# Mixture-of-experts encoder: result rows scattered to their tokens, plain loads in the combine, and another order for the first loads

## The chip, the cores and the metric

The kernel runs on one core of a Trainium2 chip. Such a core has a matrix engine (TensorE, PE in the rows), a vector engine (VectorE, DVE), a scalar engine (ScalarE, ACT), GpSimd (POOL) and a sync engine (SyncE, SP) that here only issues transfers. The engines run their own instruction lists and wait for each other through semaphores. Transfers between DRAM and the on-chip memory run on 16 DMA engines, which all queues share. In the rows, queue q1 holds what SyncE issues, q10 what ScalarE issues, and q0 what GpSimd issues.

The metric is the device time of the whole program in microseconds (us). Lower is better.

## The reference

The input is one sequence of 512 tokens with 1024 float32 values each. Two layers follow one another, and each is a mixer and a mixture of experts, with an RMS norm ahead of either:

```
for layer in range(2):
    h = rms_norm(x, norm_mix_g[layer])
    mix = hybrid_retention_s5(h, ...) if layer % 2 == 0 else windowed_gqa(h, ...)
    x = x + mix
    h = rms_norm(x, norm_ffn_g[layer])
    x = x + hier_moe(h, ...)
return rms_norm(x, norm_final_g)
```

`hier_moe` picks one of 4 groups for each token and in it the best 2 of 8 experts. An expert is `(silu(xb @ w_gate[e]) * (xb @ w_up[e])) @ w_down[e]`, with matrices of 1024x512, 1024x512 and 512x1024. The two results of a token are weighted by their gates and added to x. With 32 experts and 1024 assignments of a token to an expert, an expert has 32 tokens on average.

## The kernel before

The x matrix stays on the chip as 4 tiles of 128 tokens (`xv`). A norm (`act_norm_tile`, `dve_norm_tile`) goes tile by tile: ScalarE squares and sums, VectorE scales, ScalarE takes the root, VectorE multiplies, TensorE transposes into `hT`, and ScalarE and VectorE evacuate.

The program starts with the norm of layer 0's mixer. SyncE's list begins with one load of all of x, the constant table `c_tab`, six loads of small parameters and then the first two weight slots (`sp_mixer0`). GpSimd loads the norm's gain. After the norm TensorE makes the u projection (L1507, weights in slot 0) and z blocks (L1527), while VectorE computes the tables of the S5 part from `c_tab` and the small parameters. GpSimd starts its own part when those tables are ready. Ahead of it, GpSimd fills the rows of `y_dram` that belong to overflow blocks with ones (L2067).

In the mixture of experts (`*_moe`) each expert is one block of up to 64 tokens. 15 more overflow blocks exist for experts with more than 64 tokens, in a loop that runs no time with these inputs. All tokens' normed rows are in `h_dram`. The router (`dve_router`, `pe_router`) makes for each block the list of its tokens (`SLL`), padded with an index that is out of bounds. It does that as a product of one-hot matrices on TensorE (L397). For each block e:

- GpSimd copies the block's column of the list (L883) and issues a gather of its rows from `h_dram` (L890). Rows out of bounds are skipped.
- TensorE transposes them (L580), multiplies by gate and up (L588, L589), transposes the product (L594) and multiplies by down (L601). ScalarE and VectorE evacuate; the last evacuation (L742) makes `YE`, in which partitions 0 to 63 hold the first half of a result row and partitions 64 to 127 the second.
- ScalarE stores all 64 rows of `YE` in two transfers of 64x512 to the block's own place in `y_dram` (L871), used or not.
- SyncE loads the weights of block e+2 into the ring slots that block e has left (L795): gate and up once `e_gu` says that their matmuls are done, down once `e_dn` does. Blocks 0, 1 and 2 are loaded ahead, block 2 into places of its own. So blocks 3 and 4 are the first whose loads wait for matmuls of block 0 and 1.

When all stores have landed, GpSimd issues 8 gathers from `y_dram` (L920), one for each tile and each of the two choices, with indices that VectorE computed at the router's end (`ROWI`, L547 to L564). VectorE adds them to x (`dve_combine`, L933) and starts the next norm. SyncE has by then issued the next layer's first two weight slots (L2005).

Of the kernel before, what the change touches and what calls it, by code (L numbers as in the profile page):

```python
# [31 lines left out]
RH = 4  # L32
# [30 lines left out]
for _name, _w in [("ident", P), ("cos", NT * 64), ("sin", NT * 64), ("relp", P), ("relm", P), ("pos", 4),  # L63
                  ("before", P), ("eye16", GC), ("gtie", NGRP), ("etie", EPG), ("eid", BLK), ("bidx", MAXOV + 1),
                  ("tok", NT), ("place", BLK)]:
# [14 lines left out]
def shape_constants():  # L80
# [25 lines left out]
    put("place", (i // 4 + 16 * ((i % 4 - i // 16) % 4))[None, :])  # L106
    b = np.zeros((32, 2 * S), np.float32)
# [6 lines left out]
def encoder(nc, A, out):  # L114
    ctx = ExitStack()
    with ctx:
# [49 lines left out]
        y_dram = dram("y_dram", [NBLK * BLK, D])  # L166
# [19 lines left out]
        def spm(i):  # L186
# [4 lines left out]
        c_in, x_in, gn_in, s5_in, cc_in, b_in, moe_in = (sem(n) for n in (  # L191
            "consts_loaded", "x_loaded", "gain_loaded", "s5_rows_loaded", "s5_c_loaded", "s5_b_loaded", "router_loaded"))
        fill_st = sem("y_rows_filled")

        pe_passed, pool_passed, sp_passed = (sem(n) for n in ("pe_wait_passed", "pool_wait_passed", "sp_wait_passed"))
# [56 lines left out]
        def act_norm_tile(act, A_, n, t, ready):  # L252

            ss = small_norm(n)
            ready(act, t)
# [6 lines left out]
        NS_T = sb("norm_small", 16)  # L262
# [4 lines left out]
        def dve_norm_tile(dve, V, n, t):  # L267
# [7 lines left out]
            if t == 0:  # L275
                dve.wait_ge(gn_in, 16 * (n + 1))
# [71 lines left out]
        ROWI = INTS[:, 0:8]  # L348
# [4 lines left out]
        STG = [INTS[0:BLK, 64 + NBLK + b:65 + NBLK + b] for b in range(2)]  # L353
        assert 20 + MAXOV + 2 <= 64
# [7 lines left out]
        g_L, g_Lm, g_sl = Count("router_places"), Count("router_lists_mm"), Count("router_lists")  # L362
        xg_ld = [sem(f"x_block{b}") for b in range(2)]
# [5 lines left out]
        yk_ld = [sem(f"y_rows{i}") for i in range(8)]  # L369
# [16 lines left out]
        def pe_router(pe, l):  # L386
# [11 lines left out]
            i.then_inc(g_Lm.s, 1)  # L398

# [31 lines left out]
        def dve_router(dve, l, V):  # L431
# [98 lines left out]
            bl = shp(BL1, 8, NBLK)  # L530
            V(tv.tensor_tensor(shp(PL1, 8, BLK), ins_dim(rt("pos"), 2, BLK), ins_dim(cst("place"), 1, 8), ALU.is_equal))
            V(tv.tensor_tensor(bl, ins_dim(rt("ob"), 2, NBLK), ins_dim(cst("eid")[:, 0:NBLK], 1, 8), ALU.is_equal))
            V.sync()
            for k in range(2):
                V(tv.tensor_tensor(bl[:, NT * k:NT * (k + 1)], bl[:, NT * k:NT * (k + 1)], ins_dim(cst("tok"), 2, NBLK),
                                   ALU.mult), g_L if k else None)
            V(tv.tensor_tensor(rt("cle").rearrange("p (b e) -> p b e", e=NE), ins_dim(rt("inc"), 1, MAXOV + 1),
# [7 lines left out]

# [23 lines left out]
        def overflow_blocks(eng, l, body):  # L569

# [1590 lines left out]
```

## Time and profile before

| | us |
|---|---|
| median of 3 runs | 1761.19 |
| lowest, highest | 1756.18, 1762.73 |
| the profiled execution's own time | 1760.08 |
| its span in the profile | 1758.0 |

| engine | busy us | share of the span |
|---|---|---|
| TensorE | 1412.1 | 80% |
| VectorE | 543.7 | 31% |
| ScalarE | 247.2 | 14% |
| GpSimd | 172.9 | 10% |

The profile is of one execution. Its span is cut into stages by what runs: layer 0's mixer to about 390 us, its router to 421, its experts to 920, the combine and layer 1's mixer to 1196, the router to 1226, the experts to 1726, and the combine with the final norm to the end. A share of busy time is an average over all of them. The queues moved 486.05 MB in all, 440.26 MB of them on q1. In a timeline row the first number is the start, the second the time from the start of the first to the end of the last of the instructions merged into it, and the bracket tells how long the engine was idle before and what ended that. In a row of a DMA queue, the last number is the time that its packets took, as a share of 16 engines over the stretch that was asked for.

### The profile page before, as it was taken

To read this page: it belongs to the slowest core of one execution; us is meant where nothing else is said; L and a number is where in the kernel's file an instruction comes from. 1 tells how busy PE (TensorE), PEld (TensorE's weight loads), DVE (VectorE), ACT (ScalarE), POOL (GpSimd) and SP (SyncE) were. 2 spreads that over 40 slices of the span, in tenths; PEclk is the share of its full clock that TensorE was granted. 3 is DMA by queue.
4 is the path that set the end of the run, shared out by engine and by line. 5 is a ranking of instruction groups with operands and counts; after the bars stand their busy time and mean duration, and the time that the engine had idled before them with its cause. 6 is when DMAs were issued, how large, how long until landed. Compare 5 with 4: busy or idle time off the path is not lost. (4 is left out here: it accounts for less than half of the span.)

```text
span 1758.0 us, 18695 instructions
## 1 busy us (share of the span) xinstructions
PE 1412.1 (80%) x7013; PEld 686.5 (39%) x7013; DVE 543.7 (31%) x1125; ACT 247.2 (14%) x501; POOL 172.9 (10%) x215
## 2 busy tenths in 40 slices
PE   6999756995988878878875989894997878878872
PEld 3444745552333333323322457653333323323330
DVE  6998589124111111101114038424111101101104
ACT  2201222110100000000002027411100000000001
POOL 0007070001100000000002000001100000000002
PEclk9999877996999999989997989996999989989996
DMA  7510502426999999999996200406899999999994
GB/s 236 150 66 15 49 13 97 203 101 264 392 403 413 404 410 413 410 404 410 407 395 231 80 17 1 192 36 255 348 392 411 409 407 410 408 403 412 405 418 168
DMA packets 75027, 486.05 MB, mean 276 GB/s; under 512 B 16752, under 2 KB 23536, under 8 KB 50016
## 3 DMA queue, kind: packets, MB, share of 16 engines
q1 hardware_dynamic: 53984, 440.26, 63.5%
q0 software_dynamic: 9472, 23.94, 4.3%
q10 hardware_dynamic: 11520, 21.15, 3.2%
q8 instruction: 34, 0.56, 0.1%
q14 instruction: 17, 0.14, 0.0%
HBM read 465.91 MB, written 27.79 MB: 281 GB/s over the span
## 5 line engine op out<-in xcount | busy, mean ns | idle before, releaser
L588 PE MATMUL psum<-ring,work 128*64 128x512 f32 x992 | 494.9, 657 | 128.4 <-DMA ring<-in_moe_w_up 125.7
L589 PE MATMUL psum<-ring,work 128*64 128x512 f32 x992 | 495.9, 658 | 0.0
L588 PEld LDWEIGHTS psum<-ring,work 128*64 128x64 f32 x992 | 145.1, 151 | 449.8 <-issue 446.2
L601 PE MATMUL psum<-ring,work 128*64 128x512 f32 x992 | 226.5, 598 | 31.1 <-DVE work L739 31.1
L736 DVE TENSOR_TENSOR work<-work,psum 64x512 f32<-64x512 f32 x64 | 44.2, 690 | 639.4 <-ACT work L693 566.4
L693 ACT ACTIVATE work<-psum 64x512 f32<-64x512 f32 x64 | 37.8, 590 | 839.9 <-PE psum L589 839.9
L589 PEld LDWEIGHTS psum<-ring,work 128*64 128x64 f32 x992 | 145.0, 151 | 0.0
L601 PEld LDWEIGHTS psum<-ring,work 128*64 128x64 f32 x992 | 66.6, 136 | 145.0 <-issue 125.1
L742 DVE COPY work<-psum 128x512 f32<-128x512 f32 x64 | 44.2, 691 | 247.7 <-PE psum L601 247.7
L1527 PE MATMUL psum<-ring,hT 128*128 128x512 f32 x256 | 112.1, 600 | 2.1 <-ACT work L1646 2.1
L883 POOL COPY ints<-ints 64x1 uint32 (+1 forms) x64 | 11.4, 178 | 816.6 <-PE psum L580 772.8
L1527 PEld LDWEIGHTS psum<-ring,hT 128*128 128x128 f32 x256 | 49.0, 192 | 63.8 <-issue 63.8
L580 PE MATMUL psum<-consts,work 64*128 64x64 f32 x512 | 67.2, 272 | 7.0 <-DMA work<-h_dram,ints 7.0
L890 POOL DMA_INDIRECT work<-h_dram,ints x64 | 61.4, 959 | 54.6 <-POOL ints L883 54.6
L580 PEld LDWEIGHTS psum<-consts,work 64*128 64x128 f32 x512 | 62.7, 204 | 10.5 <-DMA work<-h_dram,ints 8.9
L308 PE MATMUL psum<-consts,work 128*128 128x128 f32 x128 | 23.7, 347 | 43.6 <-DVE work L277 43.6
L1889 PE MATMUL psum<-ring,hT 128*128 128x512 f32 x128 | 56.2, 594 | 0.5 <-issue 0.5
L1810 PE MATMUL psum<-hT,ring 128*64 128x512 f32 x256 | 55.2, 592 | 0.9 <-ACT hT L294 0.9
L594 PEld LDWEIGHTS psum<-consts,work 64*128 64x128 f32 x256 | 35.4, 210 | 51.9 <-issue 51.9
L690 ACT COPY work<-psum 128x512 f32<-128x512 f32 x64 | 37.5, 585 | 96.4 <-PE psum L580 96.4
L1853 PE MATMUL psum<-work 128*128 128x128 f32 x320 | 41.7, 288 | 5.4 <-DVE work L1987 5.4
L594 PE MATMUL psum<-consts,work 64*128 64x64 f32 x256 | 44.2, 293 | 0.0
(350 smaller groups left out, 1422.2 us busy)
## 6 DMA issues: line engine op xcount, KB each, us to landing
ring<-in_moe_w_gate SPq DMA_DIRECT2D x62, 2048.0 KB
ring<-in_moe_w_up SPq DMA_DIRECT2D x62, 2048.0 KB, 23.1
ring<-in_moe_w_down SPq DMA_DIRECT2D x62, 2048.0 KB, 23.6
y_dram<-work ACTq DMA_DIRECT2D x128, 128.0 KB
ring<-in_hyb_w_in SPq DMA_DIRECT2D x5, 2048.0 KB, 9.8
ring<-in_swa_w_qkv SPq DMA_DIRECT2D x3, 2048.0 KB, 14.3
y_dram<-ones POOLq DMA_DIRECT2D x1, 4096.0 KB, 19.9
ring<-in_hyb_w_out SPq DMA_DIRECT2D x2, 2048.0 KB, 7.7
```

The source lines that it names most:

```text
L580: i = nc.tensor.transpose(bank[b][:, c * BLK:(c + 1) * BLK], XG[b][:, c::KC], ident[0:BLK, 0:BLK])
L588: nc.tensor.matmul(bank[2 + b][0:BLK, :], XT[b][:, c, :], g[:, c, :], start=c == 0, stop=c == KC - 1)
L589: i = nc.tensor.matmul(bank[2 + b][BLK:P, :], XT[b][:, c, :], u[:, c, :], start=c == 0, stop=c == KC - 1)
L594: i = nc.tensor.transpose(bank[4 + b][:, c * BLK:(c + 1) * BLK], HD[b][:, c::HC], ident[0:BLK, 0:BLK])
L601: i = nc.tensor.matmul(bank[6 + b][BLK * hf:BLK * (hf + 1), :], HTE[b][:, c, :], d[:, c, hf * HALF:(hf + 1) * HALF], start=c == 0, stop=c ...
L736: nc.vector.tensor_tensor(HD[b], AA[b], bank[2 + b][BLK:P, :], ALU.mult).then_inc(done, 1)
L742: nc.vector.tensor_copy(YE[b], bank[6 + b][:, :]).then_inc(done, 1)
L890: pool.indirect_dma_start(XG[b], None, h_dram, bass.IndirectOffsetOnAxis(STG[b], 0), bounds_check=S - 1, oob_is_err=False).then_inc(done, 16)
L1527: x = nc.tensor.matmul(bank[i % 4], hT[:, c, t * P:(t + 1) * P], w[:, c, :], start=c == 0, stop=c == KC - 1)
L1810: x = nc.tensor.matmul(bank[i][64 * hf:64 * hf + 64, :], w[:, c, 64 * (2 * k + hf):64 * (2 * k + hf) + 64], hT[:, c, :], start=c == 0, sto ...
L1853: x = nc.tensor.matmul(bank[4 + kb][:, k * P:(k + 1) * P], SBF[it % 4][:, BAND * k + kb * P:BAND * k + (kb + 1) * P], DG[it % 2][:, k * P: ...
L1889: x = nc.tensor.matmul(b, hT[:, c, t * P:(t + 1) * P], wo[n][:, c, :], start=c == 0, stop=c == KC - 1)
```

## The change

The results of an expert no longer go to the block's own rows. `y_dram` now has a place for each token, choice and half row: 2048 rows of 512 values. The router makes a second list, `SCL`, of 128 rows for each block (partition and half row), by 16 more matmuls on TensorE whose one-hot side carries twice the token's row (`srow`). GpSimd copies the block's column and issues an indirect store, a scatter, of `YE`. Rows out of bounds are skipped. The fill with ones and the computation of `ROWI` on VectorE go. In the combine SyncE issues 8 plain loads of 128x1024.

At the start, x comes in four loads with the identity behind the first; the first norm's gain comes from ScalarE's queue; the rest of the constant table and four small parameters come from GpSimd's; two small parameters stand behind the weights. In every norm a square root of one value stands ahead of the wait for the first tile.

```
+            if t == 0:
+                A_(nc.scalar.activation(WARM, ONES[:, 0:1], ACT.Sqrt))
             ready(act, t)
...
+            bs = shp(BL2, 8, NBLK)
+            pe.wait_ge(g_S.s, l + 1)
+            for hf in range(2):
+                for a in range(8):
+                    i = nc.tensor.matmul(bank[5][BLK * hf:BLK * (hf + 1), 0:NBLK], pl[:, a, :], bs[:, a, :], start=a == 0,
+                                         stop=a == 7)
+            i.then_inc(g_Sm.s, 1)
...
+            V.sync()
+            V(tv.tensor_tensor(bs, bs, ins_dim(cst("srow"), 2, NBLK), ALU.mult), g_S)
...
-            pi, a, b = rt("q").bitcast(I32), rt("qp").bitcast(I32), rt("ei").bitcast(I32)
...
-            V(tv.tensor_copy(ROWI, rt("row")))
...
+            dve.wait_ge(g_Sm.s, l + 1)
+            V(tv.tensor_scalar(SCL, bank[5][:, 0:NBLK], cst("half"), 2.0 * NOROW, ALU.add, ALU.add), g_sc)
...
-            def store(e, par):
-                act.wait_ge(e_y, b0 + e + 1)
-                store_y1(act, par, e, y_st[par])
...
+            def scatter_y(b, done):
+
+                pool.indirect_dma_start(y_dram, bass.IndirectOffsetOnAxis(SSTG[b], 0), YE[b], None, bounds_check=4 * S - 1,
+                                        oob_is_err=False).then_inc(done, 16)
+
+            def store(e, par):
+                pool.wait_ge(e_y, b0 + e + 1)
+                col = SCL[:, e:e + 1] if isinstance(e, int) else SCL[:, bass.ds(e, 1)]
+                pool.tensor_copy(SSTG[par], col).then_inc(e_sst, 1)
+                pool.wait_ge(e_sst, b0 + e + 1)
+                pool.sem_inc(passed, 1)
+                scatter_y(par, y_st[par])
...
+            for t in range(NT):
+                for k in range(2):
+                    r0 = 2 * (S * k + P * t)
+                    sp.dma_start(YK[NT * k + t], y_dram[r0:r0 + 2 * P, :].rearrange("(p h) d -> p (h d)", h=2)).then_inc(
+                        yk_ld[t] if t + k else yk0_ld, 16)
...
-            for i in (k * NT + t for t in range(NT) for k in range(2)):
-                pool.indirect_dma_start(YK[i], None, y_dram, bass.IndirectOffsetOnAxis(ROWI[:, i:i + 1], 0)).then_inc(yk_ld[i], 16)
...
-            sp.dma_start(xv, A["x"][0].rearrange("(t p) d -> p t d", p=P)).then_inc(x_in, 16)
+            for t in range(NT):
+                sp.dma_start(xv[:, t, :], A["x"][0, t * P:(t + 1) * P, :]).then_inc(x_in[t], 16)
+                if t == 0:
+                    sp.dma_start(ident, A["c_tab"][:, 0:P]).then_inc(id_in, 16)
...
+            pool.dma_start(CT[:, P:], A["c_tab"][:, P:]).then_inc(c_in, 16)
...
-            pool.dma_start(y_dram[NE * BLK:].rearrange("(p r) (c d) -> p (r c) d", p=P, d=P), ins_dim(ONES[:, :], 1, n)).then_inc(
-                fill_st, 16)
-            pool.wait_ge(fill_st, 16)
...
+            act.dma_start(GN[:, :], bass.AP(A["norm_mix_g"].tensor, 0, [[0, P], [1, D]])).then_inc(id_in, 16)
```

SyncE's list at the start of the program, before:

```order
2 L1729 DMA x_sb<-in_x 128x4x1024
3 L1734 DMA consts<-in_c_tab 128x1204
4 L1735 DMA work<-in_s_a_re 32x128
5 L1736 DMA work<-in_s_a_im 32x128
6 L1737 DMA s_small<-in_s_log_step 32x2
7 L1738 DMA s_small<-in_ret_decay_logit 128x8
8 L1739 DMA s_small<-in_s_d 128x4x1
9 L1740 DMA s_small<-in_s_b_glu 128x4
10 L1732 DMA ring<-in_hyb_w_in 128x8x512 x2
11 L1750 DMA work<-in_s_c_re 128x1x64 x8
```

And of the changed kernel:

```order
2 L1739 DMA x_sb<-in_x 128x1024
3 L1741 DMA consts<-in_c_tab 128x128
4 L1739 DMA x_sb<-in_x 128x1024 x3
5 L1744 DMA ring<-in_hyb_w_in 128x8x512 x2
6 L1748 DMA s_small<-in_s_d 128x4x1
7 L1749 DMA s_small<-in_s_b_glu 128x4
8 L1757 DMA work<-in_s_c_re 128x1x64 x8
```

Nothing but x and the identity stands ahead of the first weights now, and x is four semaphores instead of one.

TensorE's list from the router's product to the first expert's matmuls (layer 0), before. The 64x48 matmuls make the lists, the 16x512 one belongs to layer 1's attention bias, the 128x64 ones transpose block 0's rows:

```order
141 L390 MATMUL psum<-work,ones 128x160
142 L391 MATMUL psum<-work,consts 128x128
143 L397 MATMUL psum<-work 64x48 x8
144 L2117 MATMUL psum<-work 16x512
145 L580 MATMUL psum<-consts,work 128x64 x8
```

And of the changed kernel:

```order
141 L399 MATMUL psum<-work,ones 128x160
142 L400 MATMUL psum<-work,consts 128x128
143 L406 MATMUL psum<-work 64x48 x8
144 L413 MATMUL psum<-work 64x48 x16
145 L2125 MATMUL psum<-work 16x512
146 L585 MATMUL psum<-consts,work 128x64 x8
```

The 16 matmuls of the second list stand between the first list and block 0's transposes.

GpSimd's list in the loop over the blocks (layer 0), before; one of the two halves of the loop's body:

```order
72 L883 COPY ints<-ints 64x1
73 L884 REGISTER_ALU
74 L890 DMA work<-h_dram,ints 64x1024
```

And of the changed kernel:

```order
79 L878 COPY ints<-ints 64x1
80 L879 REGISTER_ALU
81 L885 DMA work<-h_dram,ints 64x1024
82 L900 REGISTER_ALU
83 L902 ISA
84 L902 COPY ints<-work 128x1
85 L896 DMA y_dram<-work,ints 2048x512
```

The gather of block e+4 is followed by the scatter of block e, which waits for `YE` of that block.

## Rows read from the trace of the kernel before

**Rows 1.** Waits from 500 to 850 us: who waited, us in total, times, longest.

```profile
PE psum L588 <- DMA ring<-in_moe_w_up: 52.0, 19, 5.3
```

**Rows 2.** Same stretch: length, PE, PEld, DVE, ACT, POOL, PEclk, DMA share, GB/s.

```profile
500.00:850.00 350.00, 286.18 (x1298) 115.40 (x1294) 39.71 (x66) 25.87 (x44) 24.96 (x44) 0.92 1.01 409
```

**Rows 3.** DMA packets and queues from 433 to 901 us.

```profile
DMA packets 19264, 190.72 MB, mean 408 GB/s; under 512 B 3676, under 2 KB 3676, under 8 KB 8320
...
q10 hardware_dynamic: 4640, 7.61, 4.3%
...
q0 software_dynamic: 2320, 3.82, 2.5%
```

**Rows 4.** DMA queue 0 from 55 to 85 us, the fill of y_dram.

```profile
q0 software_dynamic: 1040, 4.19, 50.3%
```

**Rows 5.** GpSimd's timeline between two blocks.

```profile
504.64 0.96 POOL L890 DMA_INDIRECT work<-h_dram,ints  x1 [0.85 <-POOL ints L883]
```

**Rows 6.** Timeline of the start, to the first projection.

```profile
10.29 1.06 ACT L258 ACTIVATE work<-x_sb 128x1024 f32<-128x1024 f32 x1 [8.27 <-DMA x_sb<-in_x]
...
11.45 1.28 ACT L260 ACT_TABLE_LOAD   x1
...
13.25 1.28 DVE L277 SCALAR_TENSOR_TENSOR work<-x_sb,norm_small,norm_gain 128x1024 f32<-128x1024 f32 x1
...
18.99 1.29 DVE L277 SCALAR_TENSOR_TENSOR work<-x_sb,norm_small,norm_gain 128x1024 f32<-128x1024 f32 x1
...
23.46 29.45 PE L1507 MATMUL psum<-ring,hT 128*64 128x512 f32 x128 [0.35 <-DVE ring L1677]
```

**Rows 7.** Transfers by line, whole run: count, KB each, us from issue to landing.

```profile
h_dram<-work ACTq DMA_DIRECT2D x8, 512.0 KB, 2.6
...
norm_gain<-in_norm_mix_g POOLq DMA_DIRECT2D x2, 512.0 KB, 10.2
```

**Rows 8.** Busy time and transfers of the first 18 us.

```profile
0.00:18.00 18.00, 3.32 (x15) 3.07 (x16) 4.27 (x9) 7.44 (x13) 1.14 (x6) 1.00 0.85 311
```

**Rows 9.** VectorE's waits from 20 to 400 us, one of them.

```profile
DVE work L1196 <- PE psum L1553: 5.4, 1, 5.4
```

**Rows 10.** Timeline of layer 1's combine.

```profile
1725.20 0.69 DVE L742 COPY work<-psum 128x512 f32<-128x512 f32 x1 [3.76 <-PE psum L601]
...
1730.39 0.97 POOL L920 DMA_INDIRECT work<-y_dram,ints  x1 [60.48 <-issue]
...
1734.80 1.28 DVE L933 SCALAR_TENSOR_TENSOR x_sb<-work,x_sb 128x1024 f32<-128x1024 f32 x1 [8.91 <-DMA work<-y_dram,ints]
...
1741.93 0.15 DVE L271 TENSOR_SCALAR norm_small<-norm_small 128x1 f32<-128x1 f32 x1
```

**Rows 11.** TensorE from the router's lists to block 0, layers 0 and 1.

```profile
412.45 1.94 PE L397 MATMUL psum<-work 128*64 128x48 f32 x16 [7.75 <-DVE work L535]
...
414.32 1.89 PE L2117 MATMUL psum<-work 32*16 32x512 f32 x2
...
418.95 1.14 PE L580 MATMUL psum<-consts,work 64*128 64x64 f32 x8 [2.75 <-DMA work<-h_dram,ints]
...
1218.46 1.94 PE L397 MATMUL psum<-work 128*64 128x48 f32 x16 [7.75 <-DVE work L535]
...
1224.62 1.14 PE L580 MATMUL psum<-consts,work 64*128 64x64 f32 x8 [4.21 <-DMA work<-h_dram,ints]
```

**Rows 12.** Busy time by stretch: block 0's gate and up, slow and fast.

```profile
420.00:426.00 6.00, 5.33 (x15) 1.53 (x16) 0.00 (x0) 1.87 (x2) 1.13 (x2) 0.50 0.98 371
...
427.00:431.00 4.00, 4.00 (x20) 1.23 (x17) 0.00 (x0) 0.13 (x1) 0.00 (x0) 1.00 0.00 0
```

**Rows 13.** SyncE's first load that waits for block 0.

```profile
430.86 0.33 SPq L795 DMA_DIRECT2D ring<-in_moe_w_gate  x1
```

**Rows 14.** TensorE after an idle time in layer 0's mixer.

```profile
247.11 0.70 PE L1458 MATMUL psum<-ring,work 128*64 128x128 f32 x4 [8.36 <-DVE hT L1437]
...
252.78 1.09 PE L1464 MATMUL psum<-ring,hT 64*64 64x128 f32 x16
```

More of the change, by code:

```diff
@@ L190, in encoder @@
         w_in = [sem(f"w_loaded{i}") for i in range(6)]
[L191 to L195, printed above, removed]
+        c_in, id_in, gn_in, s5_in, cc_in, b_in, moe_in = (sem(n) for n in (
+            "consts_loaded", "ident_and_first_gain_loaded", "gain_loaded", "s5_rows_loaded", "s5_c_loaded", "s5_b_loaded", "router_loaded"))
+        passed = sem("wait_passed")
+        x_in = [sem(f"x_tile{t}_loaded") for t in range(NT)]
         class Count:
@@ L353, in encoder @@
         STG = [INTS[0:BLK, 64 + NBLK + b:65 + NBLK + b] for b in range(2)]
+        BL2 = cut(WK, 12288 + 8 * NBLK, 8 * NBLK)
+        SCL = rt("big")[:, 0:NBLK].bitcast(U32)
+        SSTG = [INTS[:, b:b + 1] for b in range(2)]
         assert 20 + MAXOV + 2 <= 64
@@ L368, in encoder @@
         y_st = [sem(f"y_stored{b}") for b in range(2)]
-        yk_ld = [sem(f"y_rows{i}") for i in range(8)]
+        yk_ld = [sem(f"y_rows{t}") for t in range(NT)]
+        yk0_ld = sem("y_rows_first")
         ov = [{k: sem(f"ov{l}_{k}") for k in ("w", "i", "xg", "xt", "xe", "gu", "a", "h", "ht", "he", "dn", "y", "st")}
@@ L720, in act_moe @@
                     xe(i * 2 + 2 + k, k)
-                    store(i * 2 + k, k)
                     silu(i * 2 + 2 + k, k)
-            for b in range(2):
-                store(NE - 2 + b, b)
             def body(j):
@@ L898, in pool_moe @@
             pool.wait_ge(h_st, 16 * NT * (l + 1))
+            def scatter_y(b, done):
[6 more added lines that the diff above has]
+                pool.wait_ge(e_sst, b0 + e + 1)
+                pool.sem_inc(passed, 1)
+                scatter_y(par, y_st[par])
             fetch(0, 0)
             fetch(1, 1)
-            with pool.Fori(0, (NE - 2) // 2) as i:
+            fetch(2, 0)
+            fetch(3, 1)
+            pool.wait_ge(g_sc.s, l + 1)
+            with pool.Fori(0, (NE - 4) // 2) as i:
                 for k in range(2):
-                    fetch(i * 2 + 2 + k, k)
+                    fetch(i * 2 + 4 + k, k)
+                    store(i * 2 + k, k)
+            for e in range(NE - 4, NE):
+                store(e, e % 2)
             def body(j):
@@ L908, in body @@
                 pool.tensor_copy(STG[1], SLL[:, bass.ds(j + NE, 1)]).then_inc(o["i"], 1)
[L909 to L910 removed]
+                pool.wait_ge(o["i"], j * 2 + 1)
+                pool.sem_inc(passed, 1)
                 gather_x(1, o["xg"])
[L912 to L926 removed]
+                pool.wait_ge(o["y"], j + 1)
+                pool.tensor_copy(SSTG[1], SCL[:, bass.ds(j + NE, 1)]).then_inc(o["i"], 1)
+                pool.wait_ge(o["i"], j * 2 + 2)
+                pool.sem_inc(passed, 1)
+                scatter_y(1, o["st"])
+                pool.wait_ge(o["st"], j * 16 + 16)
+                pool.sem_inc(passed, 1)
+            overflow_blocks(pool, l, body)
         def dve_combine(dve, l, V):
@@ L1490, in pe_mixer0 @@
         def pe_mixer0(pe):
-            pe.wait_ge(c_in, 16)
+            pe.wait_ge(id_in, 32)
             pe_norm(pe, 0)
```

115 lines of the change are left out of this document (42 added, 73 removed).

## Prediction

> **What bounds the kernel now.** I read the waits, then busy time by stretch, the DMA queues and the timelines of the seams. In the expert stages the transfers bind: from 500 to 850 us TensorE waits 19 times for an up matrix, 52.0 us in all [rows 1], the DMA share is 1.01 at 409 GB/s, and VectorE, ScalarE and GpSimd are busy for 7 to 11% [rows 2]. There a byte or packet less is time gained. Outside them, the program is a chain of engine work, in which a shift of the beginning moves everything behind it.
>
> **Scatter instead of stores.** From 433 to 901 us (468 us) 29 blocks pass: queue 10 has 58 stores, each of 64 packets of 2 KB and 16 that signal, 58 x 80 = 4640; queue 0 has 29 gathers of 64 + 16 packets, 2320 [rows 3]. 3.82 MB are 32 rows of 4 KB per gather, so a skipped row is a small packet and not nothing. The stores hold 4.3% x 468 / 29 = 0.694 us of the 16 engines per block, the gathers 2.5% x 468 / 29 = 0.403. With a for a 2 KB packet and s for a small one (a 4 KB row counted as 2a), 128a + 32s = 11.10 and 64a + 48s = 6.45 engine-us, so s = 0.028 and a = 0.080. A scatter has 64 of the one and 64 + 16 of the other: 7.36 engine-us, 0.46 us. The ends: by bytes alone 131 KB at 409 GB/s, 0.32 us; by the gather's mean packet, 0.403 x 144 / 80 = 0.725 us. The nearest row for writing to y_dram through queue 0 is the fill: 4.19 MB in 50.3% of 30 us, 236 ns per packet of 4 KB and engine [rows 4], by which a scatter would be (64 x 118 + 80 x 28) / 16 = 612 ns. I take 0.50, nearer to the packets that were measured beside the weights. 0.194 us saved x 58 blocks of both layers = **-11.3 us**; ends -21.7 and +1.8.
> The page "DMA: Bandwidth & Descriptors" of the Trainium skill, section "Bandwidth", speaks against the change: it puts a floor of some 10.5 ns on each packet of a transfer, by which a scatter's 144 packets would be 1.5 us. The trace does not bear that out: a gather's 80 packets would by it be 0.84 us and hold 0.403. By the page's figure the sum would be 58 x 0.8 = 47 us on the slow side.
> What the scatter costs GpSimd is hidden: a copy of some 0.2, a gap of 0.85 and an issue of 0.96 us [rows 5], twice per block of 16.4 us. Queued behind its wait for `YE` is the gather of block e+5, which can start only a block later in any case. The buffer of `YE` is wanted again two blocks on. ScalarE loses its issues, and it waits anyway. The fill that goes lay beside TensorE's 82 us of z projections: nothing.
>
> **The start.** Today x lands at 10.29; squaring and a table load of 1.28 put the first product at 13.25, the fourth ends at 20.28 (1.91 apart), and the projection starts 3.2 later, at 23.46 [rows 6]. Afterwards tile 0 is alone at the front: a transfer of its size takes 2.6 us [rows 7]; beside the gain's I put it at 5.0. The table load is before the wait, so the product comes 1.7 later, at 6.7, if the gain is there (10.2 us on GpSimd's queue [rows 7]; I take that it lands by 6.7 as the second of two transfers at the front). The fourth product ends at 6.7 + 1.28 + 5.73 = 13.7, and the chain allows 16.9. But slot 0's weights come behind x, the identity, the gain and the table: 5.33 MB. The first 18 us moved 311 GB/s, 5.6 MB [rows 8], at some 390 at the end, so they land at 17.3. The projection starts there: **-6.2 us**; ends -8.5 (no gap in the stream) and -3.
> It shifts what follows only if VectorE's tables come with it. They end 5.4 us before the wait on L1553 is over [rows 9]; by the same timeline TensorE gets to that product 1.6 us after they end. They need the table from GpSimd's queue, issued at about 4; by 10.2 [rows 7] it lands at 14.5, in time for 17.3. The later small parameters are not read before 70 us.
> The root ahead of the wait in the other four norms is worth nothing: their table load lies beside VectorE's two sums of the second tile, and the next root comes after these.
>
> **The combines.** Today the last `YE` is ready at 1725.89, the first gather is issued at 1730.39 and the first sum starts at 1734.80, 4.4 after the issue; the norm's step follows at 1741.93 [rows 10]. Afterwards: copy and gap make it 1727.0, the scatter lands 4.4 later at 1731.4, a plain load 2.6 later at 1734.1. The second tile waits for four loads, three more at 1.3 us (0.52 MB at 409 GB/s): 1738.0, and two sums end at 1740.6. So -1.3 for each layer, **-2.7**; ends -5 (SyncE wakes as fast as an engine) and +2 (a scatter into DRAM signals 2 us later than a gather).
>
> **The router.** On VectorE the added product of 128x384 lies in the time in which it waits for TensorE's list, and about 2 us of index arithmetic go from a place where no one waits. On TensorE 16 more matmuls, 32 instructions at 1.94 / 16 = 0.12 us: 3.9 us. In layer 0 they and L2117 (1.89) stand before block 0's transposes, which now come 2.74 after L2117's end [rows 11]: **+1.2**. In layer 1 there are 4.21 us of idle time [rows 11]: nothing.
> But TensorE's clock is 0.50 (1.2 GHz) in block 0's gate and up, 420 to 426, and 1.00 from 427 on [rows 12], after a router in which it mostly idled. The transfers stand still meanwhile (0 GB/s), since the first load that waits for block 0 is issued at 430.86 [rows 13]. So a faster block 0 starts the stream of weights earlier. At 1.00 a pair of matmuls takes about 0.43 us (some 20 matmuls in 4.00 us [rows 12]), at 0.50 twice that; the 6.3 us up to the rise hold some seven slow pairs, so 3.0 us are at stake. After the change TensorE works from 412.45 [rows 11] without a pause of over 1 us. After an idle 8.36 us the slow form lasted 5.7 us of work on narrow matmuls [rows 14], and the new work is 8 us in layer 0 and 6 in layer 1 before gate and up. So I take the fast form: **-6.0** for two layers; ends 0 and -6.5.
> The page "TensorE: Matmul & The Clock Gate", section "Part 1: The HAM clock gate", of the Trainium skill has it that recent activity, and not a count of instructions, raises the clock. Rows 14 agree; whether matmuls as small as the list's raise it, no row shows.
>
> **Sum.** -11.3 - 6.2 - 2.7 + 1.2 - 6.0 = -25.0 against the profiled execution's 1760.1 (span 1758.0 and 2.1 around it): 1735.1. It lies 1.1 under the median, so 1736 for the median.
>
> **The rivals.**
> A, the clock does not rise for the narrow matmuls, 22%: the 6.0 go, 1742. For it: the list's matmuls are small. Against: rows 14.
> B, scatters hold the engines as long as the stores did, or the rows are moved whether skipped or not (128 x 80 + 16 x 28 ns over 16 are 0.67 us), 14%: 11.3 become 0 to -1.8 the other way, about 1748. The fill's slow packets speak for it, the gathers' small ones against it.
> C, the parameters on GpSimd's queue come so late that VectorE's tables hold TensorE at 140 us, 8%: the -6.2 go, 1742. The 10.2 us of a gain on that queue speak for it.
> D, slower, 5%: the descriptors of queue 0 are dear for the engines. If a gather's 32 rows carried all of its 0.403 us, one would be 202 ns, and with 128 such a scatter 1.61 us; that is +0.92 x 58 = 53 less the other terms' 13.7, so 1800. It decides from 0.694 + 13.7 / 58 = 0.93 us per scatter on. Against it is that 48 of a gather's 80 packets move nothing and yet the whole fits in 0.403. The Trainium skill's floor per packet, named above, would land in the same place.
> The forecast itself has 48%, its own range 1729 to 1745. 3% are left for what I don't see.
>
> **Range and chances.** What a measurement here can tell from no change is 0.5%, 8.8 us. A and B together give 1754. The range 1724 to 1754 leaves out D and the outer ends. Faster by over 0.5% (under 1752.4) hold the forecast, A, C and most of B, less what is unseen: 0.83. Within 0.5%: the rest of B and combinations of A to C, 0.10. Slower: D and an unseen wait, 0.07.
>
> **What would show it.** Right: a spacing of gate loads about 0.2 us shorter (468 us for 29 blocks become about 462), queue 0 at 5.6% and queue 10 empty in that stretch, the first projection at 17.3, the step of the last combine 15 us after the last `YE`, and a clock of 1.00 in block 0's gate and up. Wrong: queue 0 above 7%, waits of TensorE for VectorE at 140 us, GpSimd's gathers later than TensorE wants them, or a combine that waits longer for SyncE's loads than for the gathers now.

## The result, and the profile after

| | before | after |
|---|---|---|
| median, us | 1761.19 | 1744.96 |
| lowest, highest of five | 1756.18, 1762.73 | 1739.70, 1748.02 |
| span of the profiled execution | 1758.0 | 1741.8 |

The ratio of the times is 0.9913, with a 95% interval from 0.9886 to 0.9940: 16.2 us faster, where 25 were forecast. The two profiled spans differ by 16.2 us too, so the two traces can be laid side by side. I cut both at the same events and took the differences:

| stretch | before | after | difference |
|---|---|---|---|
| start to the u projection | 23.46 | 19.91 | -3.55 |
| u projection to layer 0's lists | 388.99 | 388.89 | -0.10 |
| lists to block 0's gate and up | 8.32 | 8.62 | +0.30 |
| block 0's gate and up, to the first dependent load | 10.09 | 8.73 | -1.36 |
| that load to the end of the last `YE` | 487.87 | 481.95 | -5.92 |
| last `YE` to layer 1's first projection | 31.71 | 30.47 | -1.24 |
| that projection to layer 1's lists | 268.02 | 270.59 | +2.57 |
| lists to block 0's gate and up | 7.97 | 8.09 | +0.12 |
| block 0's gate and up | 10.04 | 9.87 | -0.17 |
| first dependent load to the last `YE` | 489.42 | 484.11 | -5.31 |
| last `YE` to the end | 32.11 | 30.57 | -1.54 |
| sum | 1758.00 | 1741.80 | -16.20 |

The gain sits where the scatter replaced the stores (-11.2), at the start (-3.6) and in the combines (-2.8). Block 0's two stretches, which the clock was to shorten, brought 1.5 of the 6 forecast, and a stretch that the change does not touch lost 2.6. This is one pair of profiles. Over the nine profiles of kernels with the changed TensorE list (this one and eight of the runs below), block 0's gate and up take 9.0 us on average in layer 0 (8.7 to 10.0) and 9.8 in layer 1 (8.8 to 10.1), so the 1.5 stands within some tenths; of the kernel before there is one profile.

The expert stages are bound as before, by the transfers. This is the wait of TensorE for an up matrix from 500 to 850 us:

```profile
PE psum L593 <- DMA ring<-in_moe_w_up: 52.0, 19, 4.7
```

And this the busy time by engine of that stretch (columns as in [rows 2]):

```profile
500.00:850.00 350.00, 287.57 (x1298) 115.23 (x1296) 38.63 (x64) 24.73 (x42) 51.53 (x87) 0.92 1.01 408
```

The wait is the same 52.0 us as in [rows 1], the DMA share is 1.01 again, and GpSimd is now busy for 15% instead of 7, which no other engine's wait in that stretch is put down to. What has changed is what fills the engines. These are the queues from 433 to 901 us, as in [rows 3]:

```profile
DMA packets 17858, 189.66 MB, mean 405 GB/s; under 512 B 3713, under 2 KB 3713, under 8 KB 6849
...
q1 hardware_dynamic: 13149, 181.86, 95.7%
q0 software_dynamic: 4705, 7.74, 4.8%
```

Queue 10 is empty, queue 0 has doubled its bytes, and both together fell from 6.8% to 4.8%. In the same 468 us the weights' queue moved 181.86 MB instead of 179.23.

The start, with the rows that answer to [rows 6]: the squares of the four tiles on ScalarE, the fourth product on VectorE, and the projection.

```profile
6.04 1.06 ACT L261 ACTIVATE work<-x_sb 128x1024 f32<-128x1024 f32 x1 [3.37 <-DMA x_sb<-in_x]
...
9.45 1.06 ACT L261 ACTIVATE work<-x_sb 128x1024 f32<-128x1024 f32 x1 [1.83 <-DMA x_sb<-in_x]
...
11.22 1.06 ACT L261 ACTIVATE work<-x_sb 128x1024 f32<-128x1024 f32 x1 [0.20 <-DMA x_sb<-in_x]
...
13.52 1.06 ACT L261 ACTIVATE work<-x_sb 128x1024 f32<-128x1024 f32 x1 [0.58 <-DMA x_sb<-in_x]
...
15.42 1.28 DVE L281 SCALAR_TENSOR_TENSOR work<-x_sb,norm_small,norm_gain 128x1024 f32<-128x1024 f32 x1
...
19.91 27.75 PE L1518 MATMUL psum<-ring,hT 128*64 128x512 f32 x128 [0.35 <-DVE ring L1688]
```

Each square names x as what it waited for. The tiles land 1.8 to 3.4 us apart, so the fourth product ends at 16.70, and the projection follows 3.2 us later as before. It does not wait for its weights. The first product came at 7.91, 1.2 us after the forecast's 6.7, and the fourth starts 7.5 us behind it, not 5.7.

Layer 1's combine, against [rows 10]: the last `YE`, its scatter, the loads, the first sums and the norm's step.

```profile
1710.54 0.69 DVE L740 COPY work<-psum 128x512 f32<-128x512 f32 x1 [3.76 <-PE psum L606]
...
1712.34 0.99 POOL L896 DMA_INDIRECT y_dram<-work,ints  x1 [0.86 <-POOL ints L902]
...
1715.05 4.58 SPq L865 DMA_DIRECT2D work<-y_dram  x8
...
1718.67 2.63 DVE L944 SCALAR_TENSOR_TENSOR x_sb<-work,x_sb 128x1024 f32<-128x1024 f32 x2 [7.44 <-DMA work<-y_dram]
...
1725.73 0.15 DVE L275 TENSOR_SCALAR norm_small<-norm_small 128x1 f32<-128x1 f32 x1
```

From the end of `YE` to the norm's step it is 14.5 us instead of 16.04.

The clock, in the busy times by stretch (columns as in [rows 2]): block 0's gate and up in layer 0, slow and then fast, the same in layer 1, and the first matmuls of layer 1's first projection.

```profile
417.40:420.40 3.00, 2.98 (x8) 1.01 (x10) 0.00 (x0) 1.27 (x1) 0.97 (x1) 0.50 0.90 368
421.00:425.00 4.00, 4.00 (x20) 1.26 (x18) 0.00 (x0) 0.00 (x0) 0.00 (x0) 1.00 0.34 137
1217.20:1222.20 5.00, 4.95 (x12) 1.48 (x14) 0.00 (x0) 1.28 (x1) 0.96 (x1) 0.50 0.94 384
1223.00:1227.00 4.00, 4.00 (x20) 1.12 (x16) 0.00 (x0) 0.00 (x0) 0.00 (x0) 1.00 0.02 6
938.60:942.60 4.00, 4.00 (x10) 1.34 (x12) 0.00 (x0) 0.00 (x0) 0.40 (x1) 0.50 0.84 315
```

The column of 0.50 and 1.00 is the granted clock (1.2 and 2.4 GHz). Layer 0's block 0 has 3.3 slow us instead of 6.0 [rows 12], layer 1's 5.5 instead of 5.9. The last row is new. Before the change the same matmuls ran in the fast form:

```profile
950.40:954.40 4.00, 3.96 (x20) 1.68 (x22) 0.00 (x0) 0.00 (x0) 0.78 (x2) 1.00 0.88 328
```

These are 20 matmuls in 4 us where now there are 10, though the same transposes stand ahead of them in both programs. From 938.57 to 942.9 that is 2.2 of the 2.6 us lost in that stretch. Whether it happens is not set by the program. Of the nine profiles with the changed TensorE list, five have the projection's first 3.2 to 4.4 us at 1.2 GHz and take 269.5 to 270.6 us to layer 1's lists; four have none and take 268.1 to 268.6. The kernel before took 268.0, without slow matmuls there.

### The profile page after: what moved, and what is told of

It is laid out like the page before. It is cut to its first block and busy times, and to the rows that moved or that the text cites. A ratio compares the mean times of both kernels' runs of the same rounds, so it can differ in the third digit from the quotient of the medians.

```text
span 1741.8 us, 18784 instructions
## 1 busy us (share of the span) xinstructions
PE 1416.1 (81%) x7077; PEld 689.7 (40%) x7077; DVE 542.4 (31%) x1109; ACT 247.4 (14%) x505; POOL 230.6 (13%) x330
## 5 line engine op out<-in xcount | busy, mean ns | idle before, releaser
L896 POOL DMA_INDIRECT y_dram<-work,ints x64 | 65.5, 1023 | 56.6 <-POOL ints L902 55.5
L585 PE MATMUL psum<-consts,work 64*128 64x64 f32 x512 | 67.3, 273 | 1.3 <-DMA work<-h_dram,ints 1.3
```

Source lines behind the costliest of these rows:

```text
L585: i = nc.tensor.transpose(bank[b][:, c * BLK:(c + 1) * BLK], XG[b][:, c::KC], ident[0:BLK, 0:BLK])
L896: pool.indirect_dma_start(y_dram, bass.IndirectOffsetOnAxis(SSTG[b], 0), YE[b], None, bounds_check=4 * S - 1, oob_is_err=False).then_inc(d ...
```

## The experiments

All but after_again are edits of the changed kernel. Each was timed beside the kernel before, and its ratio to that is given. "Stretch" is the time from block 0's first dependent load to the end of the last `YE`.

### ScalarE's stores again (stores_back)

```
+            def store(e, par):
+                act.wait_ge(e_y, b0 + e + 1)
+                store_y1(act, par, e, y_st[par])
...
-                    store(i * 2 + k, k)
```

> The changed kernel with ScalarE's two plain stores per block in place of the scatter, into the block's own rows; the combine's plain loads stay, so the sums take wrong rows. Theory 1 (what a block's result costs the DMA engines sets the expert stages): the two stretches from block 0's first dependent load to the last YE are 5.9 and 5.3 us longer than in the changed kernel (482 and 484 us become 488 and 489), the time is some 11 us above it, about 1756, less 1 to 2 since the last stores signal earlier than a scatter. Rival (the stages gained by something else, such as the work taken from ScalarE or the earlier start of the stream): the stretches stay at 482 and 484 and the time within 3 us of 1745.

Measured: 1757.14 us, ratio 0.9973 (0.9963 to 0.9982), and stretches of 489.66 and 489.93 us. Taking the scatter out costs 12 to 13 us against the changed kernel's two medians (1744.96, 1743.73), and the two stretches of the profiles are 13.5 longer. Theory 1 holds against the start, which stayed as changed. It does not settle ScalarE's list, since the stores are on ScalarE again here. The run with no row skipped, below, does: its ScalarE list is the light one, and its layer 0 stretch is 489.1 us, within 0.6 of the 489.66 with stores. So it is the skipped rows that made the expert stages faster.

### What a scatter's rows cost (rows_skipped, all_rows)

```
-                pool.indirect_dma_start(y_dram, ..., YE[b], None, bounds_check=4 * S - 1,
+                pool.indirect_dma_start(y_dram, ..., YE[b], None, bounds_check=0,
```

> The changed kernel in which every scatter skips all rows but at most one (its bound is 0), with y_dram filled with ones ahead under the z projections; the sums take these ones. Theory 1 (what the rows of a scatter move is what it costs, at about 0.28 us of the 16 engines per block): the expert stretches shrink by up to 0.28 x 25 = 7 us each, to 475 and 477, time 1731 to 1737. Rival A (a skipped row costs as much as a row): no change, 482 and 484, 1745. Rival B (the stretch no longer hangs on the transfers alone): less than 3 us per layer, 1739 to 1745.

```
-            V(tv.tensor_scalar(SCL, bank[5][:, 0:NBLK], cst("half"), 2.0 * NOROW, ALU.add, ALU.add), g_sc)
+            V(tv.tensor_scalar(SCL[:, 0:NE], cst("alt"), cst("half"), 0.0, ALU.add, ALU.add), g_sc)
```

> The changed kernel whose scatters skip nothing: block e writes all 128 partitions to rows 128 (e mod 16) and on; y_dram is filled with ones ahead, and the combine's sums are of no use, so only layer 0's expert stretch is read. Theory 1 (the queue's packets carry two rows each, 64 and 16 signals per scatter; rows that move cost about 0.28 us per 64 of 2 KB, of which 0.6 come back as time): the scatter's packets carry 262 KB, and the stretch from the first dependent load to the last YE is 487 to 489 us instead of 482, as far above as it was below (477.5) with all rows skipped. Rival A (packets count, not what they carry): 482. Rival B (by bytes at 409 GB/s in full, 0.32 us for each of 28 blocks): 491.

Layer 0's stretch is 477.53 us with all rows skipped (first load 427.90, last `YE` 905.43) and 489.12 with none skipped. Between them lie 481.95 in the changed kernel and 481.8 to 483.0, mean 482.4, over the six profiles of kernels with this scatter and no edit of TensorE's list. The whole time of rows_skipped, 2001 us, says nothing on the scatter: with other sums layer 1's router chose other experts, and its overflow blocks ran (gate loads 40 us apart at the end, which no other kernel has). all_rows took 1756.6 us, ratio 0.9970 (0.9957 to 0.9982).

Each of the two runs has one profile, and the six range over 1.2 us.

The queues from 440 to 880 us (packets, MB, share of 16 engines); of the changed kernel:

```profile
DMA packets 16260, 178.22 MB, mean 405 GB/s; under 512 B 3538, under 2 KB 3538, under 8 KB 5840
...
q0 software_dynamic: 4542, 7.51, 4.9%
```

with all rows skipped:

```profile
DMA packets 16428, 176.48 MB, mean 401 GB/s; under 512 B 4976, under 2 KB 4976, under 8 KB 5885
...
q0 software_dynamic: 4560, 3.74, 3.0%
```

and with none skipped:

```profile
DMA packets 16021, 179.18 MB, mean 407 GB/s; under 512 B 3060, under 2 KB 3060, under 8 KB 5760
...
q0 software_dynamic: 4480, 11.07, 6.8%
```

The packets are the same number, some 28.4 times 160: 80 for the gather, and 80 for the scatter of 128 rows, not 144. The bytes run from nothing over 131 to 262 KB per scatter, so a packet carries up to two rows, and one whose rows are both skipped is small. The sizes in the trace's packet records show it directly. In the changed kernel a scatter has some 16 data packets of 4096 bytes, 33 of 2052 and 16 of 8, and with all rows skipped all but one of the data packets have 8 bytes. In the records of this stretch a packet of 4 or 8 bytes takes 9 to 10 ns, a stored row of 2048 bytes 84 ns before the change, and a gathered row of 4096 bytes 188 ns. With the gathers' 2.6% taken off (queue 0 of the kernel before in this stretch), a scatter holds the 16 engines for 3.0 - 2.6 = 0.4% of 440 us / 28.5 = 0.06 us with no rows, 2.3% / 28.4 = 0.36 with half of them, and 4.2% / 28 = 0.66 with all. The time follows by less. The 31 scatters of a stretch are 9.3 us of engine time from none to half and 9.3 from half to all; the stretch grew by 4.9 and 6.7. Theory 1 holds in both runs, and Rival A fails in both; in all_rows the measured 489.1 lies between it and Rival B.

Where the rest of the freed time goes, the gate loads show in part. The first five gaps between them are the same before and after, 71.3 us in all: the fifth load after the first comes at

```profile
502.12 0.33 SPq L795 DMA_DIRECT2D ring<-in_moe_w_gate  x1
```

before (430.86 + 71.3), and after the change (426.15 + 71.3) at

```profile
497.40 0.33 SPq L793 DMA_DIRECT2D ring<-in_moe_w_gate  x1
```

In layer 0 these five gaps are 71.3 to 71.4 us in all 14 profiles, whatever a scatter moves. So 15% of a stretch does not hang on it. The 23 gaps behind them sum to 364.2 us with all rows skipped, to 367.9 to 369.3 in the six profiles (mean 368.5) and to 376.0 with none skipped. That is 4.4 and 7.5 us for 23 x 0.30 = 6.9 us of engine time each: 0.6 and 1.1 of it, 0.86 together. In the middle of the stretch, then, most of the freed time is gained, and part of the shortfall lies in the blocks at its front.

### The start (front_old, front_old2, table_after_x)

```
+            sp.dma_start(xv, A["x"][0].rearrange("(t p) d -> p t d", p=P)).then_inc(x_in[0], 16)
+            sp.dma_start(CT[:, :], A["c_tab"]).then_inc(c_in, 16)
...
+            gain(0)
```

> The changed kernel with the first loads as they were before (x in one load, the whole table and the small parameters on SyncE's queue, the gain on GpSimd's); scatter, combine and router as changed. Theory 1 (a shift of the start is carried through to the end): the u projection starts near 23.5 us instead of 19.9, the router's lists near 412.4 instead of 408.8, and the time is 3.6 us above the changed kernel, about 1748.6, ratio to before 0.993. Rival (the earlier start is eaten later): the time is that of the changed kernel, 1745, ratio 0.991.

> Again the changed kernel with the first loads of before, now on the same chip as the changed kernel. By the profiles seen so far its u projection starts 1.7 to 2.5 us later. Theory 1 (that shift reaches the end): 2 to 3 us above the changed kernel of this call. Rival (it does not reach the end): within 1 us of it.

```
+            pool.wait_ge(x_in[NT - 1], 16)
             pool.dma_start(CT[:, P:], A["c_tab"][:, P:]).then_inc(c_in, 16)
```

> The changed kernel with one wait more: GpSimd issues the rest of the constant table only when the fourth tile of x has landed. Theory 1 (x lands late because the table and the gain share the engines with it): the last square starts at 12 instead of 13.5 us, the u projection at 18.5 instead of 19.9, time 1.4 us below the changed kernel, about 1743.6. Rival A (the tiles' own packets set their landing): 19.9 and 1745 as before. Rival B (the table now comes too late for VectorE's own tables): VectorE waits for it, TensorE waits for VectorE near 140 us, and the time is above 1745.

With the old loads the projection starts at 22.38 in both profiles, not at 23.46, since the root ahead of the wait is still there: 1.1 us of the gain at the start are its. With the new loads it starts at 19.9 to 20.7 in eight profiles, so the new order of the loads brings 1.7 to 2.5. The end does not show them clearly. front_old took 1744.58 (ratio 0.9898, 0.9883 to 0.9913), front_old2 1745.60 (0.9897, 0.9881 to 0.9912) beside the changed kernel's 1743.73 (0.9887, 0.9872 to 0.9903). That is 1.9 us with intervals of 2.7 on either side: it fits the shift and it fits none. This stays open.

table_after_x took 1741.36 (0.9892, 0.9878 to 0.9907). That is 2.4 to 3.6 us under the changed kernel's two medians, but each was timed beside other executions of the kernel before, and by the ratios (0.9913 and 0.9887) it is not clear of them. A gain in time is not shown. Its last square, the later issue of the table, and the projection:

```profile
12.30 1.04 ACT L261 ACTIVATE work<-x_sb 128x1024 f32<-128x1024 f32 x1
...
12.33 0.55 POOL L2074 DMA_DIRECT2D consts<-in_c_tab  x1 [8.74 <-DMA x_sb<-in_x]
...
19.47 5.00 PE L1518 MATMUL psum<-ring,hT 128*64 128x512 f32 x22 [0.35 <-DVE ring L1688]
```

The fourth tile lands 1.2 us sooner once the table is out of its way, as Theory 1 had it: its square starts at 12.2 to 12.3 in all three profiles with this edit and at 13.3 to 13.5 in the eight with the new loads and without it. The projection moves by 0.4 to 1.2 us against the other profiles, and VectorE does not come to wait for the table.

### The combine (combine_gathers)

```
-                    sp.dma_start(YK[NT * k + t], y_dram[r0:r0 + 2 * P, :]...)
+                    pool.indirect_dma_start(YK[NT * k + t], None, y_dram..., bass.IndirectOffsetOnAxis(ROWI[:, ...], 0))
```

> The changed kernel with GpSimd's 8 gathers (of the same rows, by a list) in place of SyncE's 8 plain loads in the combine. Theory 1 (a plain load saves what was seen between the two first profiles): from the last YE to the first sum 10.2 us instead of 7.5 to 8.1, the norm's step 1.5 us later, both layers: 2.5 to 3 us above the changed kernel, 1746 to 1748. Rival (the wait for the last scatter is the longer part, the loads save nothing): 1744.

Measured: 1745.42, ratio 0.9913 (0.9898 to 0.9928). Layer 0's last scatter, the first two gathers and the first sum:

```profile
911.49 0.98 POOL L894 DMA_INDIRECT y_dram<-work,ints  x1 [0.86 <-POOL ints L900]
...
915.04 1.00 POOL L937 DMA_INDIRECT work<-y_dram,ints  x1 [2.57 <-DMA y_dram<-work,ints]
...
916.34 0.97 POOL L937 DMA_INDIRECT work<-y_dram,ints  x1 [0.30 <-issue]
...
918.97 1.28 DVE L949 SCALAR_TENSOR_TENSOR x_sb<-work,x_sb 128x1024 f32<-128x1024 f32 x1 [8.59 <-DMA work<-y_dram,ints]
...
927.74 0.15 DVE L275 TENSOR_SCALAR norm_small<-norm_small 128x1 f32<-128x1 f32 x1
```

From the last `YE` to the norm's step are 17.4 us here and 16.7 in layer 1, against 14.6 and 14.5 with plain loads. The eleven profiles with a scatter and plain loads range from 14.1 to 16.0, mean 14.7. The issues are 1.3 us apart, and each tile needs two. So the plain loads are worth 2.0 to 2.7 us per layer by the mean. With gathers, a scatter ahead of them costs about 1 us against the stores (16.1 before); with plain loads there is no such difference (15.05 and 14.54 in stores_back). By the profile Theory 1 holds. The time does not decide: 1745.42 lies between the two forecasts.

### The clock (after_again, warm_all, warm_fit)

> The changed kernel once more, for what differs between two executions of one kernel. Theory 1 (where TensorE's clock falls and rises is not fixed by the program): the two stretches of the expert stages (block 0's first dependent load to the last YE) are again 482 and 484 us within 1.5, while block 0's gate and up (8.7 and 9.9 us in the first profile) and the stretch from the attention's first projection to layer 1's lists (270.6) come out otherwise by 1 to 3 us. Rival (the clock follows the program): these come out within 0.3 us of the first profile. The time is 1745.

Measured: 1743.73, ratio 0.9887 (0.9872 to 0.9903). The stretches are 482.27 and 483.51 as expected. The other two came out closer than expected. Block 0 took 8.83 and 9.94 us, within 0.1 of the first profile, and the projection to layer 1's lists 269.9 instead of 270.6, which speaks for the rival. But front_old and front_old2, which are one program, differ by 1.4 between the projection and the lists of layer 1 (269.5, 268.1) and by 1.1 in layer 1's block 0 (9.85, 8.77). In front_old the projection's first 3.3 us and 5.5 us of block 0 ran at 1.2 GHz, in front_old2 none and 3.3 (block 0 of layer 1 in both). So part of the clock's steps falls otherwise from one execution to the next, by 1 to 2 us per place. The stretch from the u projection to layer 0's lists varies too (388.9 and 390.8; 390.2 and 388.4), but its time at 1.2 GHz does not go with it (83.7, 83.5, 86.4 and 87.4 us), so that cause is open. The Trainium skill has it so as well ("TensorE: Matmul & The Clock Gate", "Part 1: The HAM clock gate"): the chip's observation runs freely of the kernel's start, and the number of slow matmuls varies with the run. The pair of profiles agrees that it varies; on what it hangs, no run here shows.

```
+        def pe_dummies(n, b):
+            for _ in range(n):
+                nc.tensor.matmul(bank[b][:, :], CT[:, 0:P], CT[:, P:5 * P], start=True, stop=True)
```

> The changed kernel with matmuls on TensorE whose product nobody reads, in places where it waits: 8 and 14 in each router, 30 ahead of layer 1's first norm and 5 after its first two tiles. Theory 1 (TensorE's half clock at the start of block 0 and of the attention's first projection costs end time, since the first dependent weight load waits for block 0): clock 1.00 from the first gate matmul on, block 0's gate and up take 6.9 us instead of 8.7 and 9.9, the attention's first projection gets back 2.3 us, the router's lists 1 to 2 us each; time 6 to 9 us below the changed kernel, 1736 to 1739, ratio 0.986 to 0.988. Rival A (the transfers bind whatever block 0 does): the router parts are given back in the expert stage, only the 2.3 us stay, 1743. Rival B (the clock stays low in spite of them, or they run into the work behind them): 1745 to 1755.

Measured: 1759.27, ratio 0.9990 (0.9981 to 0.9998): Rival B. I had priced an unread matmul at 0.43 us, which is the spacing of a pair of half width; one of full width takes 0.87, and layer 0's lists came at 416.30, 7.5 us late. What the run shows of the clock is worth its time. The list's and the bias' matmuls with the first of the transposes, and then block 0:

```profile
416.30:422.30 6.00, 3.98 (x53) 3.00 (x53) 1.32 (x4) 0.00 (x0) 2.36 (x4) 1.00 0.11 31
423.90:429.40 5.50, 5.49 (x14) 1.71 (x16) 0.00 (x0) 1.25 (x1) 0.96 (x1) 0.50 0.85 352
```

Ahead of 416.30 TensorE had worked without a pause from 391.14. Then came 58 matmuls, nearly all narrow, with a wait of 2.0 us ahead of the last 8, and the clock fell at 422.9, before the first gate matmul at 423.91. In the changed kernel's layer 1 the same narrow work goes on from 1209.16 to 1216.6, with a pause of 1.3 us at 1214.1, and the clock is still 0.50 at 1222.

That is not the rule, though. The nine profiles with the changed TensorE list hold 18 such places, and in 8 of them the clock rose to 2.4 GHz 3.5 to 5.0 us after the first of the list's matmuls and fell again at block 0, from 1.4 us before its first gate matmul to 0.1 behind it. In the other 10 it stayed at 1.2 GHz into block 0. This is after_again in layer 1: the lists, their end with the transposes, and block 0.

```profile
1211.90:1215.40 3.50, 3.50 (x37) 3.50 (x38) 2.20 (x6) 0.00 (x0) 0.33 (x2) 0.50 0.40 169
1215.60:1218.80 3.20, 1.28 (x17) 1.15 (x16) 0.27 (x1) 0.00 (x0) 1.82 (x3) 1.00 0.15 33
1220.00:1225.00 5.00, 4.98 (x12) 1.48 (x14) 0.00 (x0) 1.27 (x1) 0.95 (x1) 0.50 0.93 388
```

So the same list ran both ways, and either way block 0's gate and up began at 1.2 GHz. Why the clock fell at block 0 where it had risen is not shown; in all eight a wait for the gather of 0.5 to 2.1 us stands ahead of the transposes.

> The unread matmuls once more, sized by what the last run showed (0.87 us for one of 512 columns, so now 256 columns): 8 and 15 in the router's two waits, 3 between the lists and block 0's transposes, 28 and twice 5 at layer 1's first norm. Theory 1 (wide matmuls hold the clock and the list's narrow ones do not): clock 1.00 in block 0's gate and up in both layers, 6.9 us each instead of 8.7 to 10; lists at most 1 us later than in the changed kernel and done 2 us sooner; in all 4 to 8 us below the changed kernel, 1737 to 1741. Rival A (the last 3 are too little, the clock falls again ahead of block 0): block 0 takes 9 to 10 us, and the time is 1743 to 1747. Rival B (waits filled with work push what stands behind): above 1747.

Measured: 1740.14, ratio 0.9873 (0.9857 to 0.9889), with a spread of 2.1 us where the changed kernel has 5.0. The lists come at 410.38 and 1207.09. Just ahead of block 0, in it, and its rest:

```profile
416.50:419.40 2.90, 1.84 (x12) 1.30 (x14) 0.00 (x0) 1.37 (x2) 0.87 (x3) 1.00 0.68 175
419.50:422.50 3.00, 3.00 (x10) 0.98 (x8) 0.00 (x0) 0.40 (x1) 0.54 (x1) 0.50 1.02 431
423.00:427.00 4.00, 4.00 (x22) 1.27 (x18) 0.00 (x0) 0.00 (x0) 0.00 (x0) 1.00 0.20 79
```

The clock still falls, 0.85 us into block 0 in layer 0 and 0.4 us ahead of it in layer 1, and block 0 takes 8.83 and 8.62 us. The mechanism is Rival A's, though its 9 to 10 us are not reached, and the time is Theory 1's: what was gained are the lists (2.8 us in layer 0 where they took 4.9), 1.3 us in layer 1's block 0, and the first projection of layer 1, now at full clock from 931.5 on.

### The faster edits together (best, best2)

> The two edits that were faster, together: the unread matmuls of the run before and the constant table issued behind x. Theory 1 (they add up: 3.6 and 1 to 2 us below the changed kernel): 1738 to 1739, ratio 0.9865. Rival (both only move the clock's steps, and the sum is that of one): 1740 to 1741.

> The same with 5 instead of 3 unread matmuls between the lists and block 0's transposes and one more behind the transposes. Theory 1 (the clock fell at block 0 because the gap behind the last of them was too long): clock 1.00 through block 0's gate and up, 7 us instead of 8.6 to 8.8, 1 to 3 us below the run before, 1736 to 1737. Rival A (it falls for the lists' narrow matmuls that went before): 8.6 to 8.8 again and the same time. Rival B (the added matmuls hold up block 0): above the run before.

best took 1736.55 us, ratio 0.9857 (0.9842 to 0.9872), the fastest version here: 25.3 us or 1.4% under the 1761.86 of the kernel before that was timed beside it. Its interval ends where that of after_again begins, and overlaps that of warm_fit (0.9857 to 0.9889). So that the two edits add up fits the median and is not shown. best2 took 1737.84 (0.9865, 0.9849 to 0.9880), which is not to be told from it. Its clock did what Theory 1 said in one layer of two:

```profile
417.80:421.80 4.00, 4.00 (x20) 1.43 (x22) 0.00 (x0) 1.24 (x1) 0.96 (x1) 1.00 0.92 385
1214.80:1217.10 2.30, 2.30 (x7) 0.77 (x8) 0.00 (x0) 1.04 (x1) 0.96 (x1) 0.50 0.95 401
```

Layer 0's block 0 ran fast from its first matmul and took 7.13 us; layer 1's was slow at first and took 8.41. One profile does not tell whether the six matmuls or the moment decided that.

## Why the prediction was right or wrong

The direction, the mechanism of the largest term and the range held. That the sum came within 9 us is luck in part: errors cancel inside two of its terms. The size was 25 us where 16 came.

- **The scatter, -11.3: -11.2 in the two profiles, and 12 to 13 when it was taken out again. Right in sum, and by two errors that cancel.** The step "64 of the one and 64 + 16 of the other: 7.36 engine-us" failed: a scatter has 80 packets, with up to two rows in one. It holds 0.36 us, not 0.50, so 0.33 were freed per block and not 0.194. With the forecast's rule, that time freed is time gained, this would have been -19. The runs gave back 0.53 to 0.72 of the time that was freed. Over the 23 gate loads in the middle it was 0.86. That queue 0 would be at 5.6% was wrong for the same reason (4.8%). With the right packets the solved prices give the measured sum: 16 of 4 KB, 32 of 2 KB and 32 small ones are 64 x 0.080 + 32 x 0.028 = 6.0 engine-us, 0.38 us. Singly they were less good: the packet records have 84 ns for 2 KB and 9 to 10 ns, not 28, for a small one, and a row of 4 KB was dearer than two of 2 KB (188 ns).
- **The floor of 10.5 ns per packet** in the Trainium skill ("DMA: Bandwidth & Descriptors", "Bandwidth") is worked out there from the span of one transfer of 64 packets. I had set it against 0.403 us, a share of the 16 engines' time, which is another quantity. So the gather did not contradict the Trainium skill, and the 47 us were no estimate of what the engines would be held. The run with all rows skipped shows 80 packets in 0.06 us of 16 engines, 12 ns for one on its engine.
- **The start, -6.2: -3.6.** The step that failed is the landing of the tiles: "the fourth product ends at 6.7 + 1.28 + 5.73 = 13.7" took the engines' 1.91 from before, in which all of x was there. Now the tiles land 1.8 to 3.4 us apart beside the gain and the table, and the fourth product ends at 16.70. Of the 3.0 us between, 1.2 are the first product (its tile was put at 5.0 and is squared from 6.04), and 1.8 are the pace. The weights, which I had made the limit at 17.3, were never waited for, though they were late as well (18.6 to 18.8 in the five profiles that record slot 0's landing); that 16.7 + 3.2 is the start now was in the text as what "the chain allows" with the wrong 13.7 in it. The run with the table held back confirms the cause by 1.2 us.
- **The combines, -2.7: -2.8.** The parts were off and cancel: SyncE issues 2.7 us after the scatter's issue, not 4.4, and a load takes 3.6 in place of 2.6. combine_gathers shows that the plain loads alone are worth 2.0 to 2.7 per layer.
- **The router, +1.2: +0.4.** The added matmuls took 3.2 us, not 3.9, and 2.7 of them lie in the wait for the gather, as forecast.
- **The clock, -6.0: -1.5, the largest miss.** "So I take the fast form" failed: block 0 began at 1.2 GHz in all 18 places but for 0.1 us in one. The outcome is Rival A's, its reason is not. In 8 of the 18 the clock did rise during the list's work and was down again when block 0 began, so a rise ahead of block 0 is not enough. Rows 14, on which I leaned, show a clock that rose in work that went on; they say nothing of one that has to last over the next wait. The end 0 of that term would have been the better value.
- **+2.6 that no term had:** layer 1's first projection began slow in this execution. It is the clock again, in a place that the change only shifts, slow in five of nine profiles and not in four, of the same program even (front_old slow, front_old2 not). That it came out slow here is chance, as far as these profiles show.
- **Rivals B, C and D** did not occur. D's price had an error besides: by its own premise only the 64 rows that move would cost, so its scatter would be 0.81 us, not 1.61. VectorE's tables were in time: after the change too the product of [rows 9] is awaited by VectorE, for 5.3 us, and not the other way.

```profile
DVE work L1207 <- PE psum L1564: 5.3, 1, 5.3
```

The misses are 2.6 (start), 4.5 (clock) and 2.6 (projection), less 0.8 for the router and 0.1 for the stretch from the u projection to the lists: 8.8, the difference of 25 and 16.2.

## What to carry to other kernels

Where transfers bind, price a store or a scatter by its share of the DMA engines and count on some 60% of it in time over a whole stage, and on more where the loads queue without a break (0.86 here). An indirect store that skips the empty half of its rows beat plain stores of everything, and the rows moved are what it costs. Do not put a gain on TensorE's half clock into a sum on the ground that the engine works ahead of the place: here block 0 was slow from its start, or from 0.1 us behind it, 18 times out of 18, and one list gave two clocks from one execution to the next. If waits are filled with unread matmuls, take their price at their own width (0.87 us for 512 columns at 2.4 GHz) and let them end before the wait does.

## What the runs showed that I had not expected

- An indirect store of 128 rows of 2 KB comes as 64 packets (and 16 that signal), each with up to two rows. A gather of 64 rows of 4 KB comes as 64 and 16.
- The spread between executions of one kernel (5.0 us in four of the changed kernel) may be the clock's steps in part: with unread matmuls in the waits it was 2.1 us in four. In best it was 3.5 and in best2 4.5, so this is not shown.
- Matmuls whose product nobody reads made the program 3.6 us faster (0.9887 to 0.9873, intervals that overlap, with a table held back 0.9857), and at twice the width they took all of the change's gain (0.9990).
